# Chunk buffers that wait for their own places, and attention steps for one key group

## What is computed

```python
def _windowed_gqa(q, k, v, bias, in_window, sink):      # 8 query heads, 2 key groups, head size 64
    scores = einsum("bnqkgd,bnskd->bnkgqs", qb, kb) * 64 ** -0.5     # query block of 128 against 3 key blocks
    scores = where(valid, scores + bias, -1e30)
    probs = softmax(concatenate([scores, sink_col]))[..., :-1]
    return einsum("bnkgqs,bnskd->bnqkgd", probs, vb)

def step(state, xs):                                     # delta rule, 4 heads of size 128, both directions
    v_new = u - einsum("bhcd,bhde->bhce", w, state)
    o = einsum("bhcd,bhde->bhce", q_c, state) + einsum("bhcs,bhse->bhce", qk_c, v_new)
    state = state * exp(gl) + einsum("bhcd,bhce->bhde", k_c, v_new)
...
    h = h + concatenate([attn, gdn], axis=-1) @ w_out[l]
```

## Time and profile before

| | |
|---|---|
| median of 3 runs | 2316.25 us (2315.82 to 2318.38) |
| profiled execution: time of its own | 2318.24 us |
| profiled execution: span from first to last instruction | 2316.1 us |
| mean granted TensorE clock | 0.991 |
| TensorE busy | 2256.4 us, 97%, 11389 matmuls |
| VectorE busy | 1606.4 us, 69% |
| ScalarE busy | 1111.2 us, 48% |
| GpSimd busy | 1034.5 us, 45% |
| instructions | 31264 |

### The profile page before, as it was taken

The page is one execution under the profiler, slowest core; times in us unless marked ns, Lnnn a source line. Parts: engine busy times, 40 slices in busy tenths (PEclk is TensorE's granted clock), DMA queues, the critical chain, the costliest instruction groups (busy, mean ns, idle before and its releaser), DMA issues.

```text
span 2316.1 us, 31264 instructions
## 1 busy us (share of the span) xinstructions
PE 2256.4 (97%) x11389; PEld 1785.5 (77%) x11389; DVE 1606.4 (69%) x2217; ACT 1111.2 (48%) x2008; POOL 1034.5 (45%) x643
## 2 busy tenths in 40 slices
PE   9999979898989999999999999999999999999999
PEld 6778867666868888887887777777788888888886
DVE  7865767766497555589548779878978665546745
ACT  5654155765255555544445455555623332225653
POOL 2212244444147666656866311111123775546763
PEclk9999989999999999999999999999999999999999
DMA  4113453325224444755452301111033333338654
GB/s 158 45 38 98 131 169 97 107 86 190 91 83 173 169 154 150 272 187 175 154 171 79 132 28 46 46 46 46 28 105 123 132 132 112 114 126 291 195 172 147
DMA packets 153764, 289.43 MB, mean 125 GB/s; under 512 B 34915, under 2 KB 44387, under 8 KB 153612
## 3 DMA queue, kind: packets, MB, share of 16 engines
q1 hardware_dynamic: 153612, 287.44, 37.2%
HBM read 207.88 MB, written 79.51 MB: 124 GB/s over the span
## 4 chain that ended last, share of the span: by engine, by line
PE 86%; DVE 7%; issue 3%; ACT 2%; DMA 2%; POOL 1%; SPq 0%; DVEq 0%; ACTq 0%; POOLq 0%
PE bank L625 12%; PE bank L629 12%; PE bank L857 12%; PE bank L855 12%; PE bank L853 12%; PE bank L627 12%; PE bank L702 2%; PE bank L918 2%; PE bank L949 2%; PE bank L931 1%; ACT t L991 1%; DVE t L1419 1%; PE bank L840 1%; PE bank L830 1%; DVE t L1410 1%
## 5 line engine op out<-in xcount | busy, mean ns | idle before, releaser
L2083 POOL TENSOR_TENSOR t<-t,t 128x512 fp32r<-128x512 f32 (+1 forms) x494 | 814.7, 1661 | 1078.5 <-ACT t L991 1075.3
L991 ACT ACTIVATE t<-t 128x512 fp32r<-128x512 f32 (+1 forms) x689 | 448.9, 676 | 665.9 <-PE bank L857 252.9
L625 PE MATMUL bank<-t,t 128*128 128x512 f32 x1360 | 550.0, 404 | 0.6 <-ACT t L991 0.6
L629 PE MATMUL bank<-t,t 128*128 128x512 f32 x1360 | 532.7, 392 | 3.2 <-DVE t L1419 2.7
L627 PE MATMUL bank<-t,t 128*128 128x512 f32 x1360 | 531.1, 391 | 1.5 <-POOL t L2083 1.5
L853 PE MATMUL bank<-t,t 128*128 128x512 f32 x1316 | 513.8, 390 | 9.9 <-DVE t L1803 8.3
L857 PE MATMUL bank<-t,t 128*128 128x512 f32 x1316 | 513.0, 390 | 1.5 <-DVE t L1419 1.5
L855 PE MATMUL bank<-t,t 128*128 128x512 f32 x1316 | 512.8, 390 | 1.1 <-POOL t L2083 1.1
L625 PEld LDWEIGHTS bank<-t,t 128*128 128x128 f32 x1360 | 256.4, 189 | 64.0 <-issue 12.6
L629 PEld LDWEIGHTS bank<-t,t 128*128 128x128 f32 x1360 | 255.9, 188 | 61.1 <-DVE t L1419 3.5
L627 PEld LDWEIGHTS bank<-t,t 128*128 128x128 f32 x1360 | 256.5, 189 | 55.2 <-issue 4.5
(11 more groups left out here) (250 smaller groups left out, 2684.2 us busy)
## 6 DMA issues: line engine op xcount, KB each, us to landing
...
```

Of the source, the lines that this page charges most:

```text
L625: e.matmul(ps[:, :], hi[:, w, :], XH[:, x, hs], start=k == 0, stop=False)
L629: last = e.matmul(ps[:, :], hi[:, w, :], XL[:, x, hs], start=False, stop=k == j.nk - 1)
L991: return e.activation(out, in_, ACT.Copy, **kw)
L2083: return e.tensor_tensor(out, x, high.bitcast(F32), ALU.subtract)
```

## The change

1. Buffers. `p1_left(d, i, name)` gives, from the KB at which the buffer lies (`unit_kb`), the last reader of this place in the projection: the conversion of weight tile 22 or 21 below 20 KB, the last product with tile 20, 21 or 22 below 44 KB, and half 0 or half 1 of the product with tile 22 above. The steps that write the buffers of chunks 1 and 2, and qd and rk of chunk 0, wait for this event in place of `p1_x`. `qkc` of chunks 1 to 3 waits for the stores of `kkst` and of the inverse in place of `p1_banks`, and `qkm` has a wait of its own.
2. Attention. `aqk` and `atr` become one step for each key group, and the ring `attn` becomes `attn0` and `attn1`. The steps that wait for them wait for their own group, or for both where they need both.

```diff
@@ -495,6 +495,11 @@
             return self.first[d][name]
         return self.U[d][name][i % 2]
 
+    def unit_kb(self, d, i, name):
+
+        name = {"T": "D", "P": "EB"}.get(name, name)
+        return (48 if d else 12) + 2 * ("EB", "D", "AT", "TT", "QK", "rk", "qd").index(name) + 16 * (i % 2)
+
     def norm_squares(self, d, i):
 
         return (self.U[1]["EB"][0] if d and i >= 6 else self.sqg)[:, :, :]
@@ -813,22 +818,19 @@
 
 
 
-    def aqk(n, j):
+    def aqk(n, j, g):
         s0, s1 = max(n - 1, 0), min(n + 2, 8)
-        attn_banks("aqk", n, j)
+        attn_banks("aqk", n, j, g)
         q.wait_ge(done("aq", n), *[done("evd", B.at["ka", 0, f]) for f in range(2)])
-        for g in range(2):
-            lo = 64 * g
-            last = e.matmul(banks[2 + 4 * g][:, 0:128 * (s1 - s0)], M.qaB[lo:lo + 64, j, :], M.kaF[lo:lo + 64, S - 128 * s1:S - 128 * s0], start=True, stop=True)
-        last.then_inc(*tick("aqk", n, j))
-
-    def atr(n, s):
-        attn_banks("atr", n, s)
-        q.wait_ge(done("ap", 0, n), done("ap", 1, n))
-        for g in range(2):
-            for j in range(4):
-                last = e.transpose(banks[2 + 4 * g][:, 128 * j:128 * j + 128], M.prob[n % 2][g][:, j, 128 * s:128 * s + 128], ident)
-        last.then_inc(*tick("atr", n, s))
+        lo = 64 * g
+        e.matmul(banks[2 + 4 * g][:, 0:128 * (s1 - s0)], M.qaB[lo:lo + 64, j, :], M.kaF[lo:lo + 64, S - 128 * s1:S - 128 * s0], start=True, stop=True).then_inc(*tick("aqk", n, j, g))
+
+    def atr(n, s, g):
+        attn_banks("atr", n, s, g)
+        q.wait_ge(done("ap", g, n))
+        for j in range(4):
+            last = e.transpose(banks[2 + 4 * g][:, 128 * j:128 * j + 128], M.prob[n % 2][g][:, j, 128 * s:128 * s + 128], ident)
+        last.then_inc(*tick("atr", n, s, g))
 
     def apv(n, s):
         s0, s1 = max(n - 1, 0), min(n + 2, 8)
@@ -1131,7 +1133,7 @@
         n = i if d == 0 else 7 - i
         q.wait_ge(done("qk", d, i))
         if i:
-            q.wait_ge(*[done(*x) for x in K.p1_banks], *[done("z_out", h) for h in (2, 3) if O_AT[n] >= 4])
+            q.wait_ge(*([done("z_out", h) for h in (2, 3)] if O_AT[n] >= 4 else [done("kk_out", x) for x in (5, 6, 7)] + [done("inv_out")]))
         out = M.oF[:, O_AT[n]] if i else M.unit(d, 0, "QK")[:, :, :]
         copy(out, v4(K.prep_bank("qk", d, i))).then_inc(*tick("qkc", d, i))
 
@@ -1165,9 +1167,9 @@
     def crk(d, i):
         n, ps = i if d == 0 else 7 - i, K.chain_bank("cT", d, i)
         q.wait_ge(done("cT", d, i), done("ge"))
-        if i == 0:
-            q.wait_ge(*[done(*x) for x in K.p1_x])
-        if i >= 2:
+        if i < 2:
+            q.wait_ge(*[done(*x) for x in K.p1_left(d, i, "rk")])
+        else:
             q.wait_ge(done("ckd", d, i - 2))
         for j in range(4):
             a = copy(M.unit(d, i, "rk")[:, j, :], ps[:, 128 * j:128 * j + 128], scale=G["nkds" if i else "kds"][:, n, 4 * d + j:4 * d + j + 1])
@@ -1194,7 +1196,7 @@
         e.activation(sm[:, 24:28], sm[:, 16:20], ACT.Exp).then_inc(*tick("ae", g, n))
 
     def atc(g, n, s):
-        q.wait_ge(done("atr", n, s))
+        q.wait_ge(done("atr", n, s, g))
         if s:
             q.wait_ge(done("apv", n, s - 1))
         elif n:
@@ -1473,7 +1475,7 @@
         if i >= 2:
             q.wait_ge(done("lx", d, i - 2, TOP))
         if i in (1, 2):
-            q.wait_ge(*[done(*x) for x in K.p1_x])
+            q.wait_ge(*[done(*x) for x in K.p1_left(d, i, "D")])
         elif i == 0:
             q.wait_ge(done("inv_out"))
             e.memset(M.unit(d, 0, "P")[:, :, :], 0.0)
@@ -1530,6 +1532,8 @@
             tt(QK, QK, D, ALU.mult).then_inc(*tick("qkm", d, i))
             return
         q.wait_ge(done("qkc", d, i) if i else done("qk_out", d, 0))
+        if i in (1, 2):
+            q.wait_ge(*[done(*x) for x in K.p1_left(d, i, "QK")])
         if i >= 2:
             q.wait_ge(done("co", d, i - 2))
         tt(QK, D, M.oF[:, O_AT[7 - i if d else i]] if i else QK, ALU.mult).then_inc(*tick("qkm", d, i))
@@ -1606,9 +1610,9 @@
     def am(g, n, j):
         s0, s1 = max(n - 1, 0), min(n + 2, 8)
         w, b0 = 128 * (s1 - s0), 128 * (n + 2 - s1)
-        q.wait_ge(done("aqk", n, j), done("abias", g))
+        q.wait_ge(done("aqk", n, j, g), done("abias", g))
         if n >= 2:
-            q.wait_ge(done("atr", n - 2, K.blocks(n - 2) - 1), done("ap", g, n - 2), done("ae", g, n - 2))
+            q.wait_ge(done("atr", n - 2, K.blocks(n - 2) - 1, g), done("ap", g, n - 2), done("ae", g, n - 2))
         if n == 1:
             q.wait_ge(*[done("co", x, 0) for x in range(2)], done("sc", 1, 0))
         e.tensor_tensor_reduce(out=M.prob[n % 2][g][:, j, 0:w], in0=banks[2 + 4 * g][:, 0:w], in1=M.bias[g][:, j, b0:b0 + w], scale=1.0, scalar=NEG,
@@ -2105,7 +2109,7 @@
         if i >= 2:
             q.wait_ge(done("cT", d, i - 2))
         if i in (1, 2):
-            q.wait_ge(*[done(*x) for x in K.p1_x])
+            q.wait_ge(*[done(*x) for x in K.p1_left(d, i, "TT") + K.p1_left(d, i, "T")])
         elif i == 0:
             q.wait_ge(done("whi", 21), done("wlo", 21))
         spread("TT", 1 - d)
@@ -2118,7 +2122,7 @@
         if i >= 2:
             q.wait_ge(done("co", d, i - 2))
         else:
-            q.wait_ge(*[done(*x) for x in K.p1_x])
+            q.wait_ge(*[done(*x) for x in K.p1_left(d, i, "qd")])
         q.wait_ge(part("ebx", (d, i), 1), *[done("kn", 1, h, f) for h in range(4) for f in range(2)])
         e.tensor_tensor(M.unit(d, i, "qd")[:, :, :], M.qF[:, :, c], M.unit(d, i, "EB")[:, :, :], ALU.mult).then_inc(*tick("sc", d, i))
 
@@ -2228,7 +2232,7 @@
 
     def wpair(i, r):
         if i == 0:
-            q.wait_ge(done("atr", 7, 1))
+            q.wait_ge(done("atr", 7, 1, 0), done("atr", 7, 1, 1))
         elif i == 1:
             q.wait_ge(done("whi", 30 - r), done("wlo", 30 - r))
         else:
@@ -2346,7 +2350,7 @@
         if i >= 2:
             q.wait_ge(done("lb", d, i - 2, TOP), done("sc", d, i - 2))
         if i in (1, 2):
-            q.wait_ge(*[done(*y) for y in K.p1_x])
+            q.wait_ge(*[done(*y) for y in K.p1_left(d, i, "EB")])
         elif i == 0:
             q.wait_ge(*([done("inv_out")] if d else []), done("whi", 22), done("wlo", 22))
         start(flat(M.unit(d, i, "EB")[:, :, :]), M.row_of(64 + 8 * n + 4 * d), "gcl", d, i)
@@ -2357,7 +2361,7 @@
         if i >= 2:
             q.wait_ge(done("la", d, i - 2, TOP))
         if i in (1, 2):
-            q.wait_ge(*[done(*y) for y in K.p1_x])
+            q.wait_ge(*[done(*y) for y in K.p1_left(d, i, "AT")])
         elif i == 0:
             q.wait_ge(*([done("inv_out")] if d else []), done("whi", 21), done("wlo", 21))
         start(flat(M.unit(d, i, "AT")[:, :, :]), M.row_of(8 * n + 4 * d), "bel", d, i)
@@ -2391,7 +2395,7 @@
     def aq(n):
         q.wait_ge(*[done("qa_out", j) for j in range(4)], *[done(*y) for y in K.p1_banks])
         if n:
-            q.wait_ge(*[done("aqk", n - 1, j) for j in range(4)])
+            q.wait_ge(*[done("aqk", n - 1, j, g) for j in range(4) for g in range(2)])
         start(M.qaB[:, :, :], M.qa_scr[:, :, 128 * n:128 * n + 128].rearrange("j p q -> p j q"), "aq", n)
 
     def aout(n):
@@ -2527,6 +2531,17 @@
     def set_plan(self, plan):
         self.plan = plan
 
+    def p1_left(self, d, i, name):
+
+        kb, tiles = self.mem.unit_kb(d, i, name), self.bulk.of_tile
+        if kb < 20:
+            n = 22 if kb < 16 else 21
+            return [("whi", n), ("wlo", n)]
+        if kb < 44:
+            n = [n for n in (20, 21, 22) if n % 3 == (kb - 20) // 4 % 3][0]
+            return [("mm", tiles[n][-1])]
+        return [("mm", tiles[22][0 if (kb - 44) % 4 < 2 else 1])]
+
     def first_use(self, name, *key):
         if name in ("vt", "pm", "sl"):
             return self.p3_end
@@ -2587,7 +2602,7 @@
 
         if h and k == 0:
             return [("co", 1, 6)]
-        return [("co", 1, 7)] if k < 2 else [("am", g, 7, 3) for g in range(2)] if k < 5 else [("atr", 6, 2)]
+        return [("co", 1, 7)] if k < 2 else [("am", g, 7, 3) for g in range(2)] if k < 5 else [("atr", 6, 2, 0), ("atr", 6, 2, 1)]
 
     def weight_slot(self, n):
         if n in (31, 32, 33):
@@ -3000,10 +3015,10 @@
     for n in range(8):
         r = 1.5 + n / 16
         add("sp", "aq", n, rank=6 if n else 2)
-        before = [("atr", (n - 2, K.blocks(n - 2) - 1))] if n >= 2 else []
         for j in range(4):
-            add("pe", "aqk", n, j, rank=r, ring="attn", frees=[("am", (g, n, j)) for g in range(2)], behind=before)
             for g in range(2):
+                before = [("atr", (n - 2, K.blocks(n - 2) - 1, g))] if n >= 2 else []
+                add("pe", "aqk", n, j, g, rank=r, ring=f"attn{g}", frees=[("am", (g, n, j))], behind=before)
                 add("dve", "am", g, n, j, rank=r)
         add("dve", "as1", n, rank=r)
         for g in range(2):
@@ -3012,8 +3027,8 @@
         for g in range(2):
```

(4 more changed lines are left out.)

## The result

The changed kernel takes 2327.64 us, the median of five runs (2327.03 to 2330.36), against 2316.25 us for the kernel before beside it: 1.0049 times, 95% interval 1.0038 to 1.006. It is 11.4 us slower, where 6 us less was forecast. The profiled execution has a span of 2328.1 us, 12.0 more than before, and a clock of 0.987 against 0.991.

The account below looks back on a forecast made before the run. TensorE was taken as the bound, idle mostly where it waits for VectorE after the input projections. The terms -7 + 5 - 4 = -6 us gave about 2310 us; 8-in-10 range 2302 to 2320, the forecast's own 2306 to 2313.

Parts of the forecast that it names:

- What bounds the kernel: TensorE, busy 97% of the span; worst place 300 to 350, losing 19.2 of 50 us, 5.99 of it waiting for VectorE.
- Part 1, -7: Buffers waiting only for their own place's last reader let loads and VectorE steps run earlier: -7 us, bounds -15 to +4.
- points of evidence: Early `gT_scr` loads, bias loads within 4 us of the projections' end, 6 us idle gone, end near 312.
- VectorE's side of it is 5.1 + 6.1 - 4.1 = 7.1 us: After the projections: 5.1 us of VectorE steps moved ahead, 6.1 of load waits, less 4.1 of later projection end.
- The 4.1 us: Slip of the projections' end, from preparing chunk 1 of direction 0 on TensorE ahead of the last projection products.
- The early copies of the qk products only lose a wait: Copies of the qk products, written to a free place: no effect on time.
- Pairing, +5: Attention scores: separate key-group steps lose the overlap of array row halves; half the pairs split, 7.2 us, 5 counted.
- no instruction is added: On TensorE in attention: 64 score steps instead of 32 with half the products each, flips likewise, no added instructions.
- Waiting, -4: Key groups proceeding separately could remove TensorE waits of 3.2 us for scores and 2.6 before value products: -4 us.
- upper bound of 14.4 us: Attention scores: cost if all 24 and 8 pairs split, at 0.51 and 0.27 us each.
- slower: the pairs fall apart: Rival: all 32 score pairs split and lose the row-half overlap, +8.4 us, 2324.7 us; chance of slower 0.17.
- The first sign that I named for being wrong: In the changed stretch: lower idle time with the same end, meaning that work grew because pairs split.

Follow-up runs that it names:

- e9: Kernel before with the change's buffer waits, but every engine keeping the order planned with the old waits: 2317.36 us, 1.0004.
- e12: Kernel before with only the change's buffer waits, score and flip steps as before; run again for a readable profile: 2320.10 us, 1.0016.
- e6: Kernel before with only the waits of the two loads gcl and bel loosened, compute steps waiting as before: 2326.13 us, 1.0041.
- e1: Kernel before with only the change's buffer waits, score and flip steps as before, first run: 2318.94 us, 1.0014.
- e2: Kernel before with only the attention change, one score and flip step per key group, buffer waits as before: 2332.12 us, 1.0063.
- e3: Changed kernel, but each score pair kept as one step that takes both banks; flips stay split: 2321.24 us, 1.0005 of the kernel before.
- e5: Changed kernel, but the scheduler avoids putting score steps directly behind each other, so 24 of 32 pairs are split: 2339.90 us, 1.0096 of before.
- e4: Kernel before with only the attention change, each score pair kept as one step, so only flips are split: 2322.04 us, 1.0017.
- e15: Changed kernel with score pairs kept as one step and the scheduler's TensorE delay guess 235 instead of 250 ns: 2322.18 us, 1.002 of before.
- e16: Changed kernel with the scheduler's TensorE delay guess 235 instead of 250 ns, splitting 11 of 32 pairs: 2327.07 us, 1.0045 of before.

## Why the prediction was wrong, step by step

**What bounds the kernel: right for TensorE as a whole, incomplete for this stretch.** I read the hole at 323 to 329 rightly, as VectorE's pile; it went with the new order, and not with the new waits alone (e9 keeps 6.25 us of it). I didn't ask what was late next. It was the delta rule's chain: its last `co` step moved from 541.4 to 548.8 in e12 and to 559.0 after the change.

**Part 1, -7: failed.** Its points of evidence came mostly true (loads before the last product, bias loads 0.1 us behind it, no wait of over a us for them behind it, hole gone, idle 5.0 in the first 50 us). The waits for loads had only moved ahead of the end, 3.5 and 2.6 us, and the projections ended at 315.2 and not at 312. The step that failed is "VectorE's side of it is 5.1 + 6.1 - 4.1 = 7.1 us, and VectorE is what TensorE waits for in this place": the slip is not a term of VectorE's sum, since the chain begins at the end of the projections and passes the whole slip on (7.6 us in e12, with a chain of the same 232 us). And the slip was mis-sized and made of the wrong steps. The 4.1 us were for the early unit's steps on TensorE, none of which ran ahead of the last product. The 7.0 us are two more steps of `heads` (1.8), idle time (1.8, nearly all of it chunk 0's flip at 296.18 that waits for VectorE) and a lower clock (3.4). The first goes with a term that I put at nothing: "The early copies of the qk products only lose a wait". With part 1's waits the scheduler puts the qk products of chunk 2 ahead of the last product, and with the two loads alone (e6) it doesn't; which of the other waits does it, no run separates. By the medians, part 1 measures +1.6 and +3.6 alone (e1, e12), and by e2 against after -3.4 beside part 2, which is within the intervals. All are inside my bounds of -15 to +4, and none is near -7.

**Pairing, +5: the mechanism was right and the size wrong; this is the step that decides.** Two errors partly met. The price of a split pair was worked out by columns from full-height products, 0.51 and 0.27 us; it is 0.84 and 0.63, because one group alone holds the array as long as both. That couldn't be seen in a trace in which no group was ever alone, and "by columns" was the lower bound of it, not the middle. In the number I was too high: the order splits 8 pairs, not 16. The built order has that number before any run; I estimated it instead. From e3 to after the score occupancy grows by 11.7 us. Of it, 12 lone steps of 384 columns and 4 of 256 are 12 x 0.84 + 4 x 0.63, of which half, 6.3 us, is the excess. Three adjacent ones whose second product waited (1.38, 1.31 and 1.18) make 1.3. Six score steps of 1.57 to 2.05 us between 334 and 391, in stretches with a granted clock down to 0.50, where e3 has two (1.58 and 1.10), make 3.8. The upper bound of 14.4 us should have been 24 x 0.84 + 8 x 0.63 = 25.2. In e5 the 24 split pairs make 18 x 0.84 + 6 x 0.63 = 18.9, and the measured 24.2 over e3 has five steps of 1.57 us at half the clock in it.

**Split flips: a step that was missing.** I wrote "no instruction is added" and priced the flips at nothing. As four and four they take 0.49 to 0.59 us each, where eight take 0.93 (431.56 to 432.49 before): some 0.065 for each of 44 steps, 2.9 us. Occupancy shows +2.6 and +2.8 (e4, e3 against before), and e4 measures +0.17% by the ratio, with a new order in it. Over all kernels here it is 20.6 to 22.8 with whole flips and 22.9 to 25.0 with split ones, so the size is uncertain by a us or two.

**Waiting, -4: not shown by its own mechanism.** The two waits that it was to remove, 3.2 us elsewhere before scores and 2.6 before the value products, are 2.9 and 1.7 after the change, and 2.7 us of waits before flips are new. In e2, part 2 alone, TensorE is idle for 1.3 us more than before. Idle time falls between other pairs: from e3 to after by 4.5 us, and from e15 to e16 by 6.9. But it comes only with the splits, which cost 14.6 and 13.1 us of busy time in the same pairs of kernels; with the pair kept, idle falls by 2.3 to 2.6 us against before.

**The sum.** With measured terms: e3, with its split flips and part 1, stands at +1.2 us (0.0005 of 2317), and from e3 to after busy time grows by 14.6 and idle time falls by 4.5, +10.1; together +11.3, against 11.4 measured. That the two agree to 0.1 is luck: by its median e3 stands at +3.9, and the profiled execution of the changed kernel is 2.7 us above its own median. Of the 14.6, the score steps hold 11.7; the other 2.9 are spread over other steps, at a mean clock of 0.987 for 0.988. Of the rivals, "slower: the pairs fall apart" named the mechanism and gave 2324.7. I held it to need 12 split pairs; 8 were enough. The first sign that I named for being wrong, less idle time while the work grew, is what the page shows. "For it: the scheduler doesn't know of the overlap" should have weighed more, and the range should have reached it.

**What stays open:** whether part 1 costs anything beside part 2; why the score occupancy costs 0.35 us for each us in one pair of orders and over 1 in another; and how much of a difference of up to 8 us between two orders is port collisions, ScalarE's list or the clock.
